# A hybrid encoder block: in its recurrence the low parts of the weights go from GpSimd to VectorE, and three element-wise steps are placed elsewhere

## The chip, the cores and the metric

One core of one Trainium2 chip runs the whole kernel. The metric is the device time of one execution in microseconds (us): the median over runs. The engines are named as in the profile: PE is TensorE, PEld its loading of stationary operands, DVE VectorE, ACT ScalarE, POOL GpSimd, SP SyncE, which here only issues transfers.

## What is computed

The block works on 2048 tokens of width 1024, in float32. After a normalisation one large projection feeds two mixers: latent attention, and a gated linear recurrence (branch B). Their outputs are gated and projected. The change touches branch B alone:

```python
f = lb + (1.0 - lb) * sigmoid(hf)            # lb: one lower bound for each key channel
log_f = log(f);  k_in = 1.0 - f
# for each block of tokens:
cum = cumsum(log_f)
q_dec = q * exp(cum);  k_inv = k_in * exp(-cum);  k_end = k_in * exp(last - cum)
a = where(causal, q_dec @ k_inv.T, 0)
o = a @ v + q_dec @ state                    # state carried from block to block
o = rmsnorm(o, g_hgrn)
```

With s the sigmoid, f is lb + (1 - lb) s, so that 1 - f is (1 - lb)(1 - s). The keys meet only the queries or a state that the queries read later, so a factor 1 - lb for a channel may stand on the queries as well as on the keys.

## The kernel before

Matrix products in float32 are made of three products of a high and a low part of each operand (`three_products`, lines 74 to 76): ACT rounds a tile to its high part, and another engine subtracts that from the tile to get the low part. The program has three stages, one after the other: the input projection, the recurrence with the merge logits (tiles in `bankD`, and names that begin with `d_`), and then latent projections, attention and output.

The recurrence stage is a loop over 16 units. A unit is one pair of heads (128 key channels, one on each partition) by one block of 512 tokens. Beside each unit PE works off 16 groups of three 128x512 products of the merge logits (weights `w_hi`, `w_lo`, whose two buffers are `early_w_*` and `shared_w_*`). These need no result of the recurrence and fill PE; the small products of the unit stand between them at fixed places. `PLACES` says before which group each stands: the turning of the keys (L1692) before group 0, the scores (L1682) and the state updates (L1702) before group 1, the products within a block (L1713) before group 8, those from the states (L1723) before group 9, and the turning of the outputs (L1732) before groups 11 and 12. The first unit has places of its own (`FIRST_PLACES`), later in the unit. In each engine the order is that of the code; semaphores order the engines among themselves.

One unit n on DVE: low part of the turned keys (L1606), masked scores (L1610), the lower bound for unit n + 1 (`lower_bounded`, L1568), state updates and their scan (L1622, L1629), low part of the masked scores (L1633, two instructions, which L1713 on PE waits for), low part of the states (L1635, for L1723), then for unit n + 1 the running sum of log f (`accumulated`, L1575 to L1584), the decayed queries (L1589) and the decayed keys (L1593), then the output scaling of unit n - 1 (`scaled`, L1597 by the inverse norm and L1601 by the gain), and the sums, squares and means of unit n (L1646 to L1651). ACT has the logarithm (L1477), the rounding of the weights (L1506) and of the states (L1533), exponentials (L1481 for the queries, L1490 for the keys, both into the tile `e`), and copies out of PSUM (L1539, L1544). POOL has three low parts and a copy: the weights of unit n + 1 (`split_weights`, L1429), keys and queries (L1443, L1445), values (L1437, L1439). SP loads what is needed two units ahead, once the buffer's last user has signalled, and stores the output.

Of the kernel before, what the change touches and what calls it, by code (L numbers as in the profile page):

```python
# [8 lines left out]
ALU = mybir.AluOpType  # L9
# [97 lines left out]
def input_projection(nc, plain_hi, plain_lo, sums_hi, sums_lo, shared, early, x, g_pre, w_in, b_gate, lb_logits, g_hgrn, ident_d, causal_d,  # L107
# [48 lines left out]
    with ExitStack() as ctx:  # L156
# [238 lines left out]
        with nc.Block() as block:  # L395
# [431 lines left out]
            def _(dve):  # L827
# [179 lines left out]
                dve.wait_ge(next_in, 80)  # L1007
                dve.tensor_scalar(early.f_in[:, 0], early.f_in[:, 0], span[:, 0:1], lb[:, 0:1], ALU.mult, ALU.add).then_inc(lb_step, 1)
                dve.wait_ge(lb_step, 7)

# [240 lines left out]
def merge_logits_and_recurrence(nc, hT_hi, hT_lo, shared, early, own, w_in, projT, hgTok, oB, w_ukv, g_kv):  # L1251
# [13 lines left out]
    with ExitStack() as ctx:  # L1265
# [35 lines left out]
        v_split = sem("v_split")  # L1301
        f_ready = sem("f_ready")
        ln_ready = sem("ln_ready")
# [53 lines left out]
        with nc.Block() as block:  # L1357
# [58 lines left out]
            @block.gpsimd  # L1416
            def _(pool):
                pool.sem_inc(w_split, 1)
                pool.sem_inc(v_split, 1)
                pool.memset(eps[:], EPS).then_inc(const_set, 1)  # L1420
                pool.memset(masked[:], 0.0).then_inc(const_set, 1)
                pool.memset(decay[:], 0.0).then_inc(const_set, 1)
                pool.memset(states[:], 0.0).then_inc(const_set, 1)
                pool.wait_ge(const_set, 4)
                pool.memset(decay[:, :, CPB + 1:], 1.0).then_inc(const_set, 1)

                def split_weights(n, u):
                    pool.wait_ge(w_hi_done, n + 1)
                    pool.tensor_tensor(w_lo[u], w_raw[u], w_hi[u].bitcast(F32), ALU.subtract).then_inc(w_split, 1)  # L1429

                def split_values(n, u, trips):
                    by_head = v_raw[u].rearrange("p t (h n) -> p t h n", n=VD)
                    pool.wait_ge(v_in[u], trips * 16 + 16)
                    if not is_first(n - 1):
                        pool.wait_ge(o_done, n * 2 - 2)
                    pool.sem_inc(waited_pool, 1)
                    pool.tensor_scalar(v[u][:, :, :, 0:VD], by_head, 1.0, None, ALU.mult).then_inc(v_hi, 1)  # L1437
                    pool.wait_ge(v_hi, n)
                    pool.tensor_tensor(v[u][:, :, :, VD:], by_head, v[u][:, :, :, 0:VD].bitcast(F32), ALU.subtract).then_inc(v_split, 1)  # L1439

                def split_unit(n, u):
                    pool.wait_ge(ki_hi, n + 1)
                    pool.tensor_tensor(ki[:, 1], e[:], ki[:, 0].bitcast(F32), ALU.subtract).then_inc(ki_lo, 1)  # L1443
                    pool.wait_ge(qd_hi, n + 1)
                    pool.tensor_tensor(qd[:, 1], q_in2[:, u], qd[:, 0].bitcast(F32), ALU.subtract).then_inc(qd_lo, 1)  # L1445

                split_unit(0, 0)
                split_values(1, 1, 0)
                split_weights(1, 1)
                split_unit(1, 1)  # L1450
                with pool.Fori(0, UNITS // 2 - 1) as i:
                    for u in range(2):
                        split_values(i * 2 + (u + 2), u, i + 1)
                        split_weights(i * 2 + (u + 2), u)
                        split_unit(i * 2 + (u + 2), u)

            @block.scalar
            def _(act):
# [12 lines left out]

                def log_f(n, u):
                    act.wait_ge(f_ready, n + 1)
                    act.wait_ge(ki_lo, n + 1)
                    if not is_first(n):
                        act.wait_ge(ket_turned, n)
                    act.activation(e[:], f_in2[:, u], ACT.Ln).then_inc(ln_ready, 1)  # L1477

# [34 lines left out]

                def unit(n, u, more):
                    act.wait_ge(ket_turned, n + 1)
# [13 lines left out]
                    if more:  # L1529
                        log_f(n + 1, 1 - u)  # L1530
                        round_weights(n + 1, 1 - u)
# [15 lines left out]

                log_f(0, 0)
                exp_up(0)
                act.wait_ge(const_set, 5)  # L1550
                factors(0)
                round_unit(0, 0)
                unit(0, 0, True)
                with act.Fori(0, UNITS // 2 - 1) as i:
                    for u in range(2):
                        unit(i * 2 + (u + 1), 1 - u, True)
                unit(UNITS - 1, 1, False)
                inverse_rms(UNITS - 1)
# [3 lines left out]
            def _(dve):  # L1562

                dve.sem_inc(ki_lo, 1)

                def lower_bounded(pair, u, trips):
                    dve.wait_ge(qf_in[u], trips * 32 + 32)
                    dve.tensor_scalar(f_in2[:, u], f_in2[:, u], span[:, ds(pair, 1)], lb[:, ds(pair, 1)], ALU.mult, ALU.add)\  # L1568
                       .then_inc(f_ready, 1)

# [15 lines left out]

                def decayed_q(n, u):
                    dve.wait_ge(up_ready, n + 1)
                    dve.tensor_tensor(q_in2[:, u], q_in2[:, u], e[:], ALU.mult).then_inc(q_ready, 1)  # L1589

# [3 lines left out]

                def scaled(n):
                    dve.wait_ge(rms_ready, n + 1)
                    dve.tensor_tensor(o_sum[:].rearrange("p h t n -> p (h t) n"), o_sum[:].rearrange("p h t n -> p (h t) n"),  # L1597
                                      rms[:].unsqueeze(2).to_broadcast([P, 2 * TPB, VD]), ALU.mult).then_inc(normed, 1)
                    dve.wait_ge(normed, n + 1)
                    dve.wait_ge(o_stored, n * 16 + 16)  # L1600
                    dve.tensor_tensor(o_out[:].rearrange("p t h n -> p h t n"), o_sum[:],  # L1601
                                      gain[:].unsqueeze(1).unsqueeze(1).to_broadcast([P, 2, TPB, VD]), ALU.mult).then_inc(o_ready, 1)

                def unit(pair, blk, n, more):
                    dve.wait_ge(ket_hi, n + 1)
                    dve.tensor_tensor(ket[:, 1], bank[:, B_TURN[0]], ket[:, 0].bitcast(F32), ALU.subtract).then_inc(ket_lo, 1)  # L1606
                    for hh in range(2):
# [4 lines left out]
                                            bank[:, B_SCORE + hh].rearrange("p (t n) -> p t n", n=P)).then_inc(masked_ready, 1)  # L1612
                    if more:
                        lower_bounded(pair + (blk + 1) // NB, (blk + 1) % 2, pair * (NB // 2) + (blk + 1) // 2)
                    if blk == 0:
# [21 lines left out]
                    if more:  # L1637
                        accumulated(n + 1, (blk + 1) % NB)
                        decayed_q(n + 1, (blk + 1) % 2)
                        decayed_k(n + 1, (blk + 1) % 2)  # L1640
                    if not is_first(n):
                        scaled(n - 1)
                        dve.wait_ge(o_ready, n)
# [9 lines left out]
                dve.sem_inc(w_hi_done, 1)  # L1653
                dve.sem_inc(f_ready, 1)
                dve.memset(inside[:], 1.0).then_inc(inside_set, 1)
# [5 lines left out]
                dve.wait_ge(const_set, 5)  # L1661
                decayed_q(0, 0)
                decayed_k(0, 0)
# [5 lines left out]
                for blk in range(NB):  # L1669
                    unit(PAIRS - 1, blk, (PAIRS - 1) * NB + blk, blk < NB - 1)  # L1670
                scaled(UNITS - 1)

# [1589 lines left out]
```

## Time and profile before

| | |
|---|---|
| median of 3 runs | 2312.72 us (2311.35 to 2313.54) |
| the profiled execution, by the same clock | 2310.02 us |
| its span, first to last instruction | 2308.1 us |
| PE busy | 2150.9 us (93%) |
| DVE, ACT, POOL busy | 1384.1, 1033.5, 462.5 us |
| input projection, until about | 790 us |
| recurrence stage | 790 to 1180 us |
| mean granted clock of PE, whole span | 0.962 |

The profiled execution lasted 1.9 us longer than its span. "Busy" adds up the durations of an engine's instructions; those of PE overlap by modelling, so that a busy PE isn't one at full speed. The granted clock is a share of the full 2.4 GHz: 1.00 is full, 0.50 is 1.2 GHz, and what lies between is a stretch that had both.

### The profile page before, as it was taken

Reading aid. Unit: us, or ns where it says so; the run is one execution under the profiler, and the core shown is the slowest. Engines: PE = TensorE matmul, PEld = TensorE weight load, DVE = VectorE, ACT = ScalarE, POOL = GpSimd, SP = SyncE. Lnnn points to the kernel's source line nnn. Section 1 sums busy time; section 2 is a strip of 40 time slices with the busy share of each in tenths; the row PEclk is TensorE's granted clock in tenths of the full one; section 3 lists DMA queues with packets and bytes.
Section 4 is the critical chain, followed back from the end, with each engine's and each line's share of the span. In section 5 each row is a group of like instructions: output and inputs, shape, how many; then the busy total and the mean of one; then the engine's idle time right before and its main releaser. Section 6 shows DMA issues by size and latency. Waiting matters only on the chain.

```text
span 2308.1 us, 34300 instructions
## 1 busy us (share of the span) xinstructions
PE 2150.9 (93%) x12181; PEld 1820.8 (79%) x12181; DVE 1384.1 (60%) x2192; ACT 1033.5 (45%) x1854; POOL 462.5 (20%) x395
## 2 busy tenths in 40 slices
PE   6999999999999889899978989999999998999998
PEld 5799878878998677777766768778888777778786
DVE  6633445474435466677656657677777767564652
ACT  5322335433224445455443336565666665443441
POOL 3322222442212333333311430000000022000000
PEclk9999999999999979899889999999999999999999
DMA  5432335334324223223166864333212337584651
GB/s 150 120 101 74 105 106 168 101 91 146 101 76 139 74 65 109 73 81 101 55 210 219 274 199 92 71 71 73 53 41 58 74 101 217 160 232 130 201 155 64
DMA packets 264388, 273.14 MB, mean 118 GB/s; under 512 B 38608, under 2 KB 194704, under 8 KB 261776
## 3 DMA queue, kind: packets, MB, share of 16 engines
q1 hardware_dynamic: 253776, 252.36, 38.1%
q0 software_dynamic: 5696, 10.79, 1.8%
q10 hardware_dynamic: 4800, 8.42, 1.0%
q8 instruction: 76, 1.25, 0.2%
q14 instruction: 40, 0.33, 0.0%
HBM read 178.16 MB, written 93.35 MB: 118 GB/s over the span
## 4 chain that ended last, share of the span: by engine, by line
PE 43%; DVE 8%; ACT 5%; DMA 5%; issue 4%; SPq 1%; ACTq 0%; POOL 0%; DVEq 0%; PEldq 0%; POOLq 0%
PE bankE L74 4%; PE bankE L76 3%; PE bankE L75 3%; PE scores L74 3%; PE turn_rest L2650 3%; PE scores L76 2%; PE scores L75 2%; DVE d_a_hl L1633 2%; DMA e_g_in<-gateTok 2%; PE o_acc L2662 2%; PE bankD L74 2%; PE bankD L1723 2%; PE o_acc L2663 2%; PE bankD L76 2%; PE bankD L75 2%
## 5 line engine op out<-in xcount | busy, mean ns | idle before, releaser
L2444 DVE TENSOR_REDUCE small_chunk_min<-scores 128x1 f32<-128x512 f32 (+2 forms) x320 | 181.1, 605 | 34.2 <-PE scores L76 20.0
L865 DVE TENSOR_TENSOR shared_w_lo<-shared_w_raw,shared_w_hi 128x512 fp32r<-128x512 f32 x138 | 109.2, 793 | 139.2 <-ACT shared_w_hi L666 139.0
L2464 ACT ACTIVATE probs<-scores,small_least 128x1024 f32<-128x1024 f32 (+2 forms) x192 | 167.1, 870 | 14.7 <-DVE small_least L2451 13.3
L2598 DVE TENSOR_TENSOR pT<-turn_rest,pT 128x512 fp32r<-128x512 f32 (+2 forms) x208 | 126.2, 625 | 53.0 <-ACT pT L2564 53.0
L666 ACT ACTIVATE shared_w_hi<-shared_w_raw 128x512 fp32r<-128x512 f32 x138 | 84.4, 625 | 152.8 <-POOL shared_w_raw L541 71.9
L74 PE MATMUL scores<-k_sb,q_sb 96*128 96x512 f32 (+2 forms) x320 | 127.2, 397 | 17.3 <-ACT probs L2464 14.5
L2564 ACT ACTIVATE pT<-turn_rest 128x512 fp32r<-128x512 f32 (+2 forms) x208 | 109.5, 548 | 68.9 <-PE turn_rest L2650 49.5
L1084 PE MATMUL bankA<-sums_hi,shared_w_hi 128*128 128x512 f32 x336 | 132.5, 394 | 2.4 <-DVE outs L911 1.7
L1084 PE MATMUL bankA<-sums_hi,shared_w_lo 128*128 128x512 f32 x336 | 131.0, 390 | 0.0
L1084 PE MATMUL bankA<-sums_lo,shared_w_hi 128*128 128x512 f32 x336 | 130.8, 389 | 0.0
L2662 PE MATMUL o_acc<-pT,v_sb 128*128 128x512 f32 (+1 forms) x320 | 125.2, 396 | 4.8 <-DVE pT L2598 3.9
L76 PE MATMUL scores<-k_sb,q_sb 96*128 96x512 f32 (+2 forms) x320 | 119.9, 375 | 0.0
L75 PE MATMUL scores<-k_sb,q_sb 96*128 96x512 f32 (+2 forms) x320 | 119.5, 374 | 0.0
L2663 PE MATMUL o_acc<-pT,v_sb 128*128 128x512 f32 (+1 forms) x320 | 113.3, 366 | 0.0
L74 PE MATMUL bankE<-e_uT,e_wb_hi 128*128 128x512 f32 x256 | 100.9, 394 | 8.7 <-DVE e_wb_lo L3051 6.4
L1084 PE MATMUL bankA<-plain_hi,shared_w_hi 128*128 128x512 f32 x252 | 100.1, 397 | 7.6 <-ACT outs L743 5.1
L2650 PE MATMUL turn_rest<-small_ident,probs 128*128 128x128 f32 x736 | 104.3, 278 | 0.1
L74 PE MATMUL bankE<-e_wo_hi,e_mT 128*128 128x512 f32 x256 | 101.0, 395 | 3.1 <-DVE e_wo_lo L3058 3.1
L76 PE MATMUL bankE<-e_wo_hi,e_mT 128*128 128x512 f32 x256 | 100.2, 391 | 0.0
L2967 POOL TENSOR_TENSOR e_second_branch<-e_second_branch 128x512 f32<-128x512 f32 x4 | 5.1, 1282 | 474.3 <-DMA e_second_branch<-gateTok 474.1
L75 PE MATMUL bankE<-e_wo_lo,e_mT 128*128 128x512 f32 x256 | 100.1, 391 | 0.0
L76 PE MATMUL bankE<-e_uT,e_wb_lo 128*128 128x512 f32 x256 | 99.7, 390 | 0.0
(353 smaller groups left out, 6246.0 us busy)
## 6 DMA issues: line engine op xcount, KB each, us to landing
shared_w_raw<-in_w_in_dram SPq DMA_DIRECT2D x96, 256.0 KB, 3.1
projT<-outs SPq DMA_DIRECT2D x96, 256.0 KB, 2.4
e_l_in<-projT SPq DMA_DIRECT2D x64, 256.0 KB, 4.9
t_raw<-in_w_in_dram SPq DMA_DIRECT2D x24, 512.0 KB, 4.3
x_tile<-in_x_dram SPq DMA_DIRECT2D x16, 512.0 KB, 4.8
projT<-d_stage ACTq DMA_DIRECT2D x32, 256.0 KB, 2.9
knT<-b_out SPq DMA_DIRECT2D x32, 256.0 KB, 3.5
vTok<-b_out SPq DMA_DIRECT2D x32, 256.0 KB, 4.0
```

Source lines behind the costliest of these rows:

```text
L74: pe.matmul(out, a_hi, b_hi, start=first, stop=False)
L75: pe.matmul(out, a_hi, b_lo, start=False, stop=False)
L76: return pe.matmul(out, a_lo, b_hi, start=False, stop=last)
L865: dve.tensor_tensor(slot_lo(u, i), operand(u, i), slot_hi(u, i).bitcast(F32), ALU.subtract).then_inc(w_ready, 1)
L1084: last = pe.matmul(bank[:, b], a[:, k], c[:, k], start=opens and k == 0 and a is wh and c is hh, stop=k == KH - 1 and a is wl, skip_group_ ...
L2444: dve.tensor_reduce(chunk_min[:, i % 2, c:c + 1], scores[:, s_bank(i, c), 0:width(i, c)], AX.X, ALU.min)\
L2464: act.activation(probs[b][:, r, first * BLK:first * BLK + n], src, ACT.Exp, bias=least[:, i % 2:i % 2 + 1], scale=-1.0, accum_out=sums[:, ...
L2564: act.activation(pT[:, at % RING, 0, r0 * P:], turn[TURN_AT[tile] % TURN_RING][:, r0 * P:], ACT.Copy)\
L2598: dve.tensor_tensor(pT[:, at % RING, 1, r0 * P:], turn[TURN_AT[tile] % TURN_RING][:, r0 * P:], pT[:, at % RING, 0, r0 * P:].bitcast(F32), ...
L2650: last = pe.transpose(turn[at % TURN_RING][:, r * P:(r + 1) * P], probs[b][:, r, j * P:(j + 1) * P], ident[:])
L2662: pe.matmul(dst, v_sb[u][:, j], pT[:, at % RING, 0, r0 * P:], start=j == 0, stop=False)
L2663: pe.matmul(dst, v_sb[u][:, j], pT[:, at % RING, 1, r0 * P:], start=False, stop=j == end)\
```

## The change

Four edits, all for the recurrence stage:

1. `split_weights` leaves POOL. DVE does it, as one instruction of 128x1024, right behind the decayed keys.
2. `lower_bounded` is gone, from DVE's unit and once from the end of the input projection. The input tile keeps the sigmoid s. ACT's logarithm gets the lower bound as per-partition scale and bias, and waits for the input itself. The decayed queries are multiplied by `span`, 1 - lb, in the same instruction, which becomes a scalar_tensor_tensor. The decayed keys are computed from s with the instruction as before.
3. `scaled` is cut in two: the scaling by the inverse norm stands ahead of the decayed queries, that by the gain between decayed queries and decayed keys.
4. ACT's loop, which was over two units seven times, is now over the four blocks of a pair of heads, twice, with the first and the last pair written out, since scale and bias need the number of the pair.

```diff
@@ GpSimd
-                def split_weights(n, u):
-                    pool.wait_ge(w_hi_done, n + 1)
-                    pool.tensor_tensor(w_lo[u], w_raw[u], w_hi[u].bitcast(F32), ALU.subtract).then_inc(w_split, 1)
...
                     for u in range(2):
                         split_values(i * 2 + (u + 2), u, i + 1)
-                        split_weights(i * 2 + (u + 2), u)
                         split_unit(i * 2 + (u + 2), u)
@@ ScalarE
-                def log_f(n, u):
-                    act.wait_ge(f_ready, n + 1)
+                def log_f(pair, n, u, trips):
+                    act.wait_ge(qf_in[u], trips * 32 + 32)
                     act.wait_ge(ki_lo, n + 1)
                     if not is_first(n):
                         act.wait_ge(ket_turned, n)
-                    act.activation(e[:], f_in2[:, u], ACT.Ln).then_inc(ln_ready, 1)
+                    act.sem_inc(waited_act, 1)
+                    act.activation(e[:], f_in2[:, u], ACT.Ln, scale=span[:, ds(pair, 1)], bias=lb[:, ds(pair, 1)]).then_inc(ln_ready, 1)
@@ VectorE
-                def lower_bounded(pair, u, trips):
-                    dve.wait_ge(qf_in[u], trips * 32 + 32)
-                    dve.tensor_scalar(f_in2[:, u], f_in2[:, u], span[:, ds(pair, 1)], lb[:, ds(pair, 1)], ALU.mult, ALU.add)\
-                       .then_inc(f_ready, 1)
...
-                    dve.tensor_tensor(q_in2[:, u], q_in2[:, u], e[:], ALU.mult).then_inc(q_ready, 1)
+                    dve.scalar_tensor_tensor(q_in2[:, u], q_in2[:, u], span[:, ds(pair, 1)], e[:], ALU.mult, ALU.mult).then_inc(q_ready, 1)
...
+                def split_weights(n, u):
+                    dve.wait_ge(w_hi_done, n + 1)
+                    dve.tensor_tensor(w_lo[u], w_raw[u], w_hi[u].bitcast(F32), ALU.subtract).then_inc(w_split, 1)
...
-                    if more:
-                        lower_bounded(pair + (blk + 1) // NB, (blk + 1) % 2, pair * (NB // 2) + (blk + 1) // 2)
...
                     if more:
                         accumulated(n + 1, (blk + 1) % NB)
-                        decayed_q(n + 1, (blk + 1) % 2)
+                    if not is_first(n):
+                        scaled_by_rms(n - 1)
+                    if more:
+                        decayed_q(pair + (blk + 1) // NB, n + 1, (blk + 1) % 2)
+                    if not is_first(n):
+                        scaled_by_gain(n - 1)
+                    if more:
                         decayed_k(n + 1, (blk + 1) % 2)
+                        split_weights(n + 1, (blk + 1) % 2)
                     if not is_first(n):
-                        scaled(n - 1)
                         dve.wait_ge(o_ready, n)
```

DVE's queue in the second half of the second unit, before. The names are the tiles written and read: `d_cum` the running sum, `early_q_in` the queries, `d_e` the keys, `d_o_sum` and `d_o_out` the output.

```order
L1635 TENSOR_TENSOR d_s_hl<-d_states,d_s_hl 128x8x64
L1575 SCALAR_TENSOR_TENSOR d_cum<-d_inside,d_carry,d_e 128x512
L1580 COPY d_gsum<-d_cum 128x8
L1581 COPY d_carry<-d_cum 128x1
L1584 TENSOR_TENSOR d_cum<-d_cum,d_gsum 128x8x32
L1589 TENSOR_TENSOR early_q_in<-early_q_in,d_e 128x512
L1593 SCALAR_TENSOR_TENSOR d_e<-early_f_in,d_e 128x512
L1597 TENSOR_TENSOR d_o_sum<-d_o_sum,d_rms 128x512
L1601 TENSOR_TENSOR d_o_out<-d_o_sum,shared_gain 128x2x4x64
L1646 TENSOR_TENSOR d_o_sum<-bankD,d_o_lo 128x256 x2
L1649 TENSOR_TENSOR d_o_lo<-d_o_sum 128x512
```

The same place of the changed kernel, whose line numbers differ:

```order
L1628 TENSOR_TENSOR d_s_hl<-d_states,d_s_hl 128x8x64
L1564 SCALAR_TENSOR_TENSOR d_cum<-d_inside,d_carry,d_e 128x512
L1569 COPY d_gsum<-d_cum 128x8
L1570 COPY d_carry<-d_cum 128x1
L1573 TENSOR_TENSOR d_cum<-d_cum,d_gsum 128x8x32
L1590 TENSOR_TENSOR d_o_sum<-d_o_sum,d_rms 128x512
L1578 SCALAR_TENSOR_TENSOR early_q_in<-early_q_in,shared_small,d_e 128x512
L1596 TENSOR_TENSOR d_o_out<-d_o_sum,shared_gain 128x2x4x64
L1582 SCALAR_TENSOR_TENSOR d_e<-early_f_in,d_e 128x512
L1586 TENSOR_TENSOR early_w_lo<-early_w_raw,early_w_hi 128x1024
L1645 TENSOR_TENSOR d_o_sum<-bankD,d_o_lo 128x256 x2
L1648 TENSOR_TENSOR d_o_lo<-d_o_sum 128x512
```

The two scalings have moved up, one on either side of the decayed queries, and the weights' low part stands where they stood.

POOL's loop body for one unit, before: values, weights, keys, queries.

```order
L1437 TENSOR_SCALAR early_v<-early_v_raw 128x8x64
L1439 TENSOR_TENSOR early_v<-early_v_raw,early_v 128x8x64
L1428 REGISTER_ALU
L1429 TENSOR_TENSOR early_w_lo<-early_w_raw,early_w_hi 128x1024
L1443 TENSOR_TENSOR d_ki<-d_e,d_ki 128x512
L1445 TENSOR_TENSOR d_qd<-early_q_in,d_qd 128x512
```

And in the changed kernel:

```order
L1429 TENSOR_SCALAR early_v<-early_v_raw 128x8x64
L1431 TENSOR_TENSOR early_v<-early_v_raw,early_v 128x8x64
L1434 REGISTER_ALU
L1435 TENSOR_TENSOR d_ki<-d_e,d_ki 128x512
L1437 TENSOR_TENSOR d_qd<-early_q_in,d_qd 128x512
```

The instruction of 128x1024 between values and keys is gone from POOL, and nothing takes its place.

## Rows read from the trace of the kernel before

**Rows 1.** The page: span and number of instructions.

```profile
span 2308.1 us, 34300 instructions
```

**Rows 2.** Stretches of the recurrence: length, PE busy, granted clock, DMA share, GB/s.

```profile
822.68:1159.58 336.90, 309.15 (x2184) 0.88 0.30 86
990.37:1016.54 26.17, 24.18 (x157) 0.80 0.41 122
1016.54:1038.00 21.46, 19.49 (x157) 1.00 0.17 47
1159.58:1178.67 19.09, 19.09 (x156) 1.00 0.12 40
```

**Rows 3.** Waits from 822.68 us on: us in total, times, longest.

```profile
PE bankD L1713 <- DVE d_a_hl L1633: 27.8, 14, 2.0
```

**Rows 4.** PE's timeline, unit from 1016.54: start, us, instruction, idle before.

```profile
1017.77 1.56 PE L1682 MATMUL bankD<-d_qd,d_ki 64*128 64x128 f32 x24
...
1025.28 0.39 PE L76 MATMUL bankD<-plain_hi,shared_w_lo 128*128 128x512 f32 x1
1027.63 2.00 PE L1713 MATMUL bankD<-d_a_hl,d_v 128*128 128x128 f32 x16 [1.97 <-DVE d_a_hl L1633]
...
1030.31 1.97 PE L1723 MATMUL bankD<-d_qd,d_s_hl 64*128 64x64 f32 x32
...
1033.70 0.60 PE L1732 MATMUL bankD<-shared_ident,d_o_fm 128*128 128x128 f32 x4
```

**Rows 5.** DVE's timeline in the same unit.

```profile
1019.49 1.35 DVE L1610 COPY_PREDICATED d_masked<-shared_causal,bankD 128x512 f32<-128x512 int32 x2 [0.99 <-PE bankD L1682]
1020.73 0.53 DVE L1568 TENSOR_SCALAR early_f_in<-early_f_in,shared_small 128x512 f32<-128x512 f32 x1
...
1022.73 1.49 DVE L1629 TENSOR_TENSOR_SCAN d_states<-d_states,d_decay 128x640 f32<-128x640 f32 x1 [0.20 <-ACT d_states L1526]
1024.14 3.44 DVE L1633 TENSOR_TENSOR d_a_hl<-d_masked,d_a_hl 128x512 fp32r<-128x512 f32 x2
...
1031.14 0.69 DVE L1589 TENSOR_TENSOR early_q_in<-early_q_in,d_e 128x512 f32<-128x512 f32 x1 [0.70 <-ACT d_e L1481]
1032.53 0.69 DVE L1593 SCALAR_TENSOR_TENSOR d_e<-early_f_in,d_e 128x512 f32<-128x512 f32 x1 [0.70 <-ACT d_e L1490]
...
1035.88 0.43 DVE L1646 TENSOR_TENSOR d_o_sum<-bankD,d_o_lo 128x256 f32<-128x256 f32 x1 [0.43 <-ACT d_o_lo L1544]
```

**Rows 6.** POOL's timeline in the same unit.

```profile
1024.33 2.70 POOL L1429 TENSOR_TENSOR early_w_lo<-early_w_raw,early_w_hi 128x1024 fp32r<-128x1024 f32 x1 [8.77 <-ACT early_w_hi L1506]
1034.20 1.59 POOL L1443 TENSOR_TENSOR d_ki<-d_e,d_ki 128x512 fp32r<-128x512 f32 x1 [7.18 <-ACT d_ki L1496]
```

**Rows 7.** DVE and PE in the last unit, timeline from 1159 us.

```profile
1162.50 1.36 DVE L1610 COPY_PREDICATED d_masked<-shared_causal,bankD 128x512 f32<-128x512 int32 x2 [0.96 <-PE bankD L1682]
...
1165.76 1.49 DVE L1629 TENSOR_TENSOR_SCAN d_states<-d_states,d_decay 128x640 f32<-128x640 f32 x1 [0.65 <-ACT d_states L1526]
1167.17 1.27 DVE L1633 TENSOR_TENSOR d_a_hl<-d_masked,d_a_hl 128x512 fp32r<-128x512 f32 x2
...
1168.30 0.39 PE L76 MATMUL bankD<-plain_hi,shared_w_lo 128*128 128x512 f32 x1
1168.53 1.97 PE L1713 MATMUL bankD<-d_a_hl,d_v 128*128 128x128 f32 x16
```

**Rows 8.** ACT's timeline in the unit from 1016.54.

```profile
1024.25 1.20 ACT L1533 ACTIVATE d_s_hl<-d_states 128x512 fp32r<-128x512 f32 x1
...
1032.53 1.09 ACT L1539 ACTIVATE d_o_fm<-bankD 128x512 f32<-128x512 f32 x2
```

**Rows 9.** Durations in ns, min/median/max, by tile and by line, 785 to 1200 us.

```profile
L1584 DVE TENSOR_TENSOR d_cum<-d_cum,d_gsum x16: 424/426/427, 792.4 to 1146.8; 128x256 f32<-128x256 f32 x16
...
L1464 ACT ACTIVATE d_stage<-bankD,shared_small x32: 681/686/690, 822.1 to 1179.2; 128x512 f32<-128x512 f32 x32
```

**Rows 10.** PE in the first unit, timeline.

```profile
809.85 3.67 PE L1713 MATMUL bankD<-d_a_hl,early_v 128*128 128x128 f32 x16 [4.65 <-DVE d_a_hl L1633]
```

More of the change, by code:

```diff
@@ L1007, in _ @@
                 dve.wait_ge(next_in, 80)
-                dve.tensor_scalar(early.f_in[:, 0], early.f_in[:, 0], span[:, 0:1], lb[:, 0:1], ALU.mult, ALU.add).then_inc(lb_step, 1)
-                dve.wait_ge(lb_step, 7)
             @block.tensor
@@ L1301, in merge_logits_and_recurrence @@
         v_split = sem("v_split")
-        f_ready = sem("f_ready")
         ln_ready = sem("ln_ready")
@@ L1417, in _ @@
             def _(pool):
-                pool.sem_inc(w_split, 1)
                 pool.sem_inc(v_split, 1)
@@ L1448, in _ @@
                 split_values(1, 1, 0)
-                split_weights(1, 1)
                 split_unit(1, 1)
@@ L1512, in inverse_rms, with unit @@
                     act.activation(rms[:], logm[:], ACT.Exp, scale=-0.5).then_inc(rms_ready, 1)
-                def unit(n, u, more):
+                def unit(pair, blk, n, more):
+                    u = blk % 2
                     act.wait_ge(ket_turned, n + 1)
@@ L1529, in unit @@
                     if more:
-                        log_f(n + 1, 1 - u)
+                        log_f(pair + (blk + 1) // NB, n + 1, 1 - u, pair * (NB // 2) + (blk + 1) // 2)
                         round_weights(n + 1, 1 - u)
@@ L1546, in unit @@
                     logits(n, 0)
-                log_f(0, 0)
+                log_f(0, 0, 0, 0)
                 exp_up(0)
@@ L1552, in _ @@
                 round_unit(0, 0)
[L1553 to L1557, printed above, removed]
+                for blk in range(NB):
+                    unit(0, blk, blk, True)
+                with act.Fori(1, PAIRS - 1) as pair:
+                    for blk in range(NB):
+                        unit(pair, blk, pair * NB + blk, True)
+                for blk in range(NB):
+                    unit(PAIRS - 1, blk, (PAIRS - 1) * NB + blk, blk < NB - 1)
                 inverse_rms(UNITS - 1)
@@ L1585, in accumulated, with decayed_q @@
                        .then_inc(mid_ready, 1)
-                def decayed_q(n, u):
+                def decayed_q(pair, n, u):
                     dve.wait_ge(up_ready, n + 1)
-                    dve.tensor_tensor(q_in2[:, u], q_in2[:, u], e[:], ALU.mult).then_inc(q_ready, 1)
+                    dve.scalar_tensor_tensor(q_in2[:, u], q_in2[:, u], span[:, ds(pair, 1)], e[:], ALU.mult, ALU.mult).then_inc(q_ready, 1)
                 def decayed_k(n, u):
@@ L1593, in decayed_k, with scaled_by_rms @@
                     dve.scalar_tensor_tensor(e[:], f_in2[:, u], 1.0, e[:], ALU.subtract, ALU.mult).then_inc(kd_ready, 1)
-                def scaled(n):
+                def split_weights(n, u):
+                    dve.wait_ge(w_hi_done, n + 1)
+                    dve.tensor_tensor(w_lo[u], w_raw[u], w_hi[u].bitcast(F32), ALU.subtract).then_inc(w_split, 1)
+                def scaled_by_rms(n):
                     dve.wait_ge(rms_ready, n + 1)
@@ L1598, in scaled, with scaled_by_gain @@
                                       rms[:].unsqueeze(2).to_broadcast([P, 2 * TPB, VD]), ALU.mult).then_inc(normed, 1)
+                def scaled_by_gain(n):
                     dve.wait_ge(normed, n + 1)
@@ L1653, in _ @@
                 dve.sem_inc(w_hi_done, 1)
-                dve.sem_inc(f_ready, 1)
+                dve.sem_inc(w_split, 1)
                 dve.memset(inside[:], 1.0).then_inc(inside_set, 1)
@@ L1661, in _ @@
                 dve.wait_ge(const_set, 5)
-                decayed_q(0, 0)
+                decayed_q(0, 0, 0)
                 decayed_k(0, 0)
@@ L1670, in _ @@
                     unit(PAIRS - 1, blk, (PAIRS - 1) * NB + blk, blk < NB - 1)
-                scaled(UNITS - 1)
+                scaled_by_rms(UNITS - 1)
+                scaled_by_gain(UNITS - 1)
             @block.tensor
```

## The prediction

> **What bounds the kernel now.** I began with the page, whose span is 2308.1 us [rows 1], and cut it into stages, since every edit stands in the recurrence, 790 to 1180 us. There I asked which wait ends last on PE, the engine with the most work. The table of waits gives one of weight: from 822.68 us on PE waits 14 times for the low part of the masked scores (DVE, L1633), 27.8 us in all [rows 3]. The 15th unit after the first has no such wait.
>
> Then I cut the stage at the turning of the keys, the start of a unit on PE. From 822.68 to 1159.58 us there are 14 units in 336.90 us, 24.06 each, at a mean granted clock of 0.88 [rows 2]. They are of two kinds. Six last 21.5 us at clock 1.00, like the one from 1016.54; the other eight last (336.90 - 6 x 21.46) / 8 = 26.0 us on average, like the one from 990.37 with 26.17 at 0.80 [rows 2]. The clock goes to 1.2 GHz only right behind the wait for L1633, in those eight. So a unit loses twice: the wait itself, and in eight of 14 units a stretch at half clock.
>
> Next the wait's cause, in the unit from 1016.54. PE's last large product ahead of L1713 starts at 1025.28; they follow each other every 0.23 us, so PE is free at 1025.51, and L1713 starts at 1027.63 [rows 4]: 2.12 us lost. DVE's two subtractions start at 1024.14 and end at 1027.58, 3.44 us for two [rows 5]. At 1024.33 POOL begins the weights' low part and runs 2.70 us, to 1027.03 [rows 6]. In the last unit no weights are left to split and there is no lower bound to apply: the same two subtractions take 1.27 us, and L1713 starts at 1168.53, 0.23 us behind the product before it, with no wait [rows 7]. This is the changed unit nearly as it will be, already in the trace. Its L1713 comes at the clock 1.00, and the clock stays there to the end of the unit [rows 2].
>
> **The change part by part.** *Weights' low part off POOL.* With L1633 at 1.27 instead of 3.44, the scores' low part ends 2.17 us earlier. From the start of L1610 to the end of L1633 the fast unit takes 1027.58 - 1019.49 = 8.09 us, the last unit 1168.44 - 1162.50 = 5.94 [rows 5, 7]. So in the unit from 1016.54 it would end at 1025.43, and PE is free at 1025.51. The 2.12 us go, and what is left of slack is 0.08 us: it just fits.
>
> *Lower bound gone.* Its 0.53 us [rows 5] are worth nothing on this path: the scan behind it waits for ACT's state updates, 0.20 us with it and 0.65 us in the last unit without it [rows 5, 7]. At the end of the input projection the one instruction lies beside ACT's last work; nothing. On ACT the logarithm gets two per-partition operands. The trace has none such; The nearest rows are an activation of the same shape without operands (half of 1.09 us for two, in rows that overlap, so at least 0.55 [rows 8]) and one with a per-partition bias, 0.69 [rows 9]. The bounds are 0.55 and 0.8, and I take 0.69; the old logarithm takes about 0.6. Behind it in ACT's queue is the rounding of the states, which ends at 1025.45 [rows 8]; the states' low part takes 1.0 us from there, and PE wants it 2.68 us behind the start of L1713 [rows 4], at 1028.2. That is 1.7 us of slack, and 0.1 is hidden in it. The wait for the input in place of DVE's signal costs nothing: the loads are issued two units ahead.
>
> *Output scaling.* Two instructions of about 0.69 us stand in the two gaps of 0.70 us in which DVE waits for ACT's exponentials [rows 5]. They fill them exactly; between 0 and 0.1 us of delay each. Behind stand the decayed keys, on whose heels ACT's copy of the outputs follows. In the fast unit that copy starts at 1032.53 and its first half is ready at about 1033.1, while the turning of the outputs starts at 1033.70 [rows 4, 8]: 0.6 us of slack, and both sides move up by the same 2.1 us. Hidden.
>
> *Weights' low part on DVE.* A subtraction of 256 elements takes 0.43 us [rows 9], one of 512 takes 0.69 [rows 5], so 1024 take 0.69 + 2 x 0.26 = 1.2; bounds are 1.2 and POOL's 2.70 [rows 6]. I take 1.2. It starts at 1033.2 - 2.1 = 1031.1 and ends at 1032.3. Queued behind it is the second sum of the outputs, which started at 1035.88 [rows 5], now 1033.8 (the first 0.9 us earlier): hidden, even at 1.7 us. If it took 2.7 us, the first sum would be late by 0.9 and the second not; PE wants them at the next unit's start, 1035.9, when they have been done for 1.7 us. PE needs the weights then too: 3.6 us of slack. SP loads into the raw buffer once the split has signalled; that load stood behind the store of the output, which itself waited for the scaling by the gain, and both can now go out earlier.
>
> *POOL.* Its keys' low part starts at 1034.20 and takes 1.59 us [rows 6]; one for the queries follows, up to 1.6 more: done by 1037.4, now by 1035.3. The scores of the next unit want it at 1036.0 + 1.23 = 1037.2 [rows 4]: 1.9 us of slack. Can the new subtraction on DVE hold these up? The row says that a DVE subtraction and POOL's can't run beside each other: L1633 took 3.44 us where 1.27 is its own time, and ended 0.55 us behind POOL's end [rows 5, 6]. Moved up with the rest, POOL starts at 1032.1 and DVE ends at 1032.3: POOL loses 0.2 of its 1.9 us. The Trainium skill (SBUF — State Buffer, "Who interferes with whom") has this as a rule: a DVE instruction with two SBUF inputs and a GpSimd instruction that reads SBUF share a port, and whichever starts first holds it for the whole instruction. It speaks against the edit, since the weights' subtraction still has two SBUF inputs, and by it the loss is moved rather than removed; by the rule the sum is less only if POOL's slack is used up, which the rows deny.
>
> *Sum.* 14 units of 2.12 us are 29.7 us. Half clock: 336.90 - 14 x 21.46 = 36.5 us; if no wait is left ahead of L1713, all of it goes. Together 66.1 us: 14 units of 24.06 become 19.34, and the last unit's 19.09 plus 0.23 is 19.32 [rows 2]. The first unit: PE waited 4.65 us [rows 10]; DVE's pair was just as slow there, so 2.15 us go, but 2.5 remain, and I leave the half clock behind it (3.67 us for L1713). Total 68.3 us. Profiled execution: 2310.0 - 68.3 = 2241.7. Its time stands 2.7 us under the median of the runs, 2312.7, so by the median 2244.4; I say 2244.
>
> **The rivals.** *Half clock stays in some units.* For: behind L1713 and L1723 PE has 48 small products in 4.6 us that stream little, and nothing shows that the wait alone turned the clock down; six of 14 units with the same wait kept it. Against: the last unit, and 48 small products of the scores and updates at each unit's start, behind which the clock never fell. Each such unit costs 36.5 / 8 = 4.6 us; five give 2267, all eight 2281. Chance 0.14.
>
> *The wait goes elsewhere.* Either ACT or DVE is late by more than its slack (0.08 us at L1713, 0.6 at L1732), by the filled gaps or added register work. A wait of 1 us in each unit, with no clock loss, costs 14: 2258; one as long as that removed leaves it at 2313. Chance 0.1, of which 0.02 for no change.
>
> *It doesn't do what it says:* L1633 was slow for another reason than POOL. The last unit also lacks the lower bound and the next unit's work. Against: the end of L1633 follows POOL's end by 0.55 us, and POOL has nothing else there. It would give 2313. Chance 0.02.
>
> *Slower.* ACT's logarithm with two per-partition operands is far dearer than its rows. It stands in front of the states' rounding; its delay reaches PE at L1723 beyond 1.7 us, and is as bad as the old loss (66.1 / 14 = 4.7 us a unit) from 6.4 us on; at 7.5 us it gives 2313 + 14 x 1.1 = 2328. The rows say 0.55 to 0.8. Chance 0.02, with anything else that ends above.
>
> **How the numbers follow.** The likeliest case, 0.72, is 2244, its own range 2239 (the first unit keeps its clock too) to 2250 (0.4 us of small delays a unit). For 8 in 10 I reach to five units with half clock: 2238 to 2267. 0.2% is 4.6 us, about what a measurement of this kernel can tell from no change. Faster is the likeliest, the clock rival and most of the moved wait, 0.95; same 0.03; slower 0.02.
>
> **What would show it.** Right: L1633's successor at 0.68 us for each of its two, PE without a wait ahead of the products within a block, units of 19.3 to 19.5 us, a granted clock of 1.00 from the second unit on, the weights' subtraction on DVE at 1.2 us, POOL's keys at 1.3 to 1.6. Wrong: units of two kinds at clock 0.8 and 1.0 (first rival), a wait of PE for the copied or summed outputs or the states (second), or a logarithm over 0.8 us (last).

## The result and the profile after

| | before | changed |
|---|---|---|
| median | 2312.03 us (2307.65 to 2313.54, 4 runs) | 2241.47 us (2236.52 to 2249.32, 4 runs) |
| ratio, 95% interval | | 0.9701 (0.9667 to 0.9735) |
| span of the profiled execution | 2308.1 us | 2247.5 us |
| its own time | 2310.02 us | 2249.32 us |

The kernel is 70.6 us faster by the medians, and 60.7 us by the profiled executions; that of the changed kernel is the slowest of its four. The page of the changed kernel, its head and section 1 (busy us, share, instructions):

```profile
span 2247.5 us, 34185 instructions
PE 2119.2 (94%) x12181; PEld 1797.7 (80%) x12181; DVE 1364.3 (61%) x2191; ACT 1033.7 (46%) x1854; POOL 425.1 (19%) x380
```

PE has the same 12181 instructions. Its busy time fell by 32 us only, since what left is partly idle time. The stretches of its recurrence, each cut at the turning of the keys as in [rows 2] (length, PE busy, granted clock, DMA share, GB/s):

```profile
818.91:843.72 24.81, 24.81 (x157) 0.76 0.35 93
843.72:1094.98 251.26, 251.26 (x2030) 1.00 0.35 102
1017.65:1037.01 19.36, 19.36 (x157) 1.00 0.38 109
```

From 843.72 to 1094.98 us stand 13 units of 19.33 us at a granted clock of 1.00, with PE busy from end to end. In [rows 2] a unit had 24.06 us on average. One unit, the second, is still long. In the timelines of PE, DVE, ACT and POOL for the unit from 1017.65, the answers to [rows 4 to 6] and [rows 8] are:

```profile
1026.38 0.39 PE L76 MATMUL bankD<-plain_hi,shared_w_lo 128*128 128x512 f32 x1
1026.61 1.99 PE L1713 MATMUL bankD<-d_a_hl,d_v 128*128 128x128 f32 x16
...
1023.86 1.49 DVE L1622 TENSOR_TENSOR_SCAN d_states<-d_states,d_decay 128x640 f32<-128x640 f32 x1 [0.65 <-ACT d_states L1518]
1025.27 1.27 DVE L1626 TENSOR_TENSOR d_a_hl<-d_masked,d_a_hl 128x512 fp32r<-128x512 f32 x2
1026.69 1.11 DVE L1628 TENSOR_TENSOR d_s_hl<-d_states,d_s_hl 128x512 fp32r<-128x512 f32 x1 [0.16 <-ACT d_s_hl L1525]
...
1030.41 0.75 DVE L1578 SCALAR_TENSOR_TENSOR early_q_in<-early_q_in,shared_small,d_e 128x512 f32<-128x512 f32 x1 [0.21 <-ACT d_e L1472]
1031.87 0.69 DVE L1582 SCALAR_TENSOR_TENSOR d_e<-early_f_in,d_e 128x512 f32<-128x512 f32 x1
1032.48 1.22 DVE L1586 TENSOR_TENSOR early_w_lo<-early_w_raw,early_w_hi 128x1024 fp32r<-128x1024 f32 x1
1035.32 1.32 DVE L1648 TENSOR_TENSOR d_o_lo<-d_o_sum 128x512 f32<-128x512 f32 x1
...
1023.80 0.82 ACT L1468 ACTIVATE d_e<-early_f_in,shared_small 128x512 f32<-128x512 f32 x1
...
1033.54 1.30 POOL L1435 TENSOR_TENSOR d_ki<-d_e,d_ki 128x512 fp32r<-128x512 f32 x1 [13.63 <-ACT d_ki L1487]
1034.80 1.29 POOL L1437 TENSOR_TENSOR d_qd<-early_q_in,d_qd 128x512 fp32r<-128x512 f32 x1
```

The two subtractions for the scores (now L1626) take 1.27 us and end at 1026.54. L1713 starts 0.23 us behind the product ahead of it, without a wait, and 0.07 us behind their end. The scan of the states waits 0.65 us for ACT, as in the last unit of before [rows 7]: what the lower bound had taken became waiting. The weights' subtraction takes 1.22 us on DVE, and POOL's keys start 0.16 us before its end by this profile. The logarithm on ACT takes 0.82 us, more than I had allowed; it pushes the states' low part back by 0.16 us, which is hidden. POOL idles 13.63 us ahead of the keys.

The contention isn't gone from the unit. The square of the outputs (L1648) has two inputs in SBUF too. Here it takes 1.32 us where 0.69 is its own time (in the run with the first edit alone, below), and ends 0.55 us behind the end of POOL's queries (1036.64 against 1036.09). PE doesn't wait for it.

### The profile page after: what moved, and what is told of

Read it like the earlier page. It is cut to its first block, busy times and chain, and to the rows that moved or that the text cites. A ratio compares the mean times of both kernels' runs of the same rounds, so it can differ in the third digit from the quotient of the medians.

```text
span 2247.5 us, 34185 instructions
## 1 busy us (share of the span) xinstructions
PE 2119.2 (94%) x12181; PEld 1797.7 (80%) x12181; DVE 1364.3 (61%) x2191; ACT 1033.7 (46%) x1854; POOL 425.1 (19%) x380
## 4 chain that ended last, share of the span: by engine, by line
PE 46%; DMA 5%; DVE 4%; ACT 4%; issue 3%; SPq 1%; POOL 1%; ACTq 0%; DVEq 0%; POOLq 0%
PE bankE L74 4%; PE bankE L76 4%; PE bankE L75 4%; PE scores L74 3%; PE bankD L74 3%; PE turn_rest L2650 3%; PE scores L75 3%; PE scores L76 3%; PE bankD L76 3%; PE bankD L75 3%; PE o_acc L2662 2%; PE o_acc L2663 2%; DMA e_g_in<-gateTok 2%; PE turn_first L2650 2%; ACT probs L2464 1%
## 5 line engine op out<-in xcount | busy, mean ns | idle before, releaser
L74 PE MATMUL scores<-k_sb,q_sb 96*128 96x512 f32 (+2 forms) x320 | 129.3, 404 | 20.2 <-ACT probs L2464 15.0
L76 PE MATMUL scores<-k_sb,q_sb 96*128 96x512 f32 (+2 forms) x320 | 121.6, 380 | 0.0
L75 PE MATMUL scores<-k_sb,q_sb 96*128 96x512 f32 (+2 forms) x320 | 121.6, 380 | 0.0
L74 PEld LDWEIGHTS scores<-k_sb,q_sb 96*128 96x128 f32 x320 | 63.5, 198 | 45.8 <-ACT probs L2464 29.3
```

The lines of the kernel that those rows point to most:

```text
L74: pe.matmul(out, a_hi, b_hi, start=first, stop=False)
L75: pe.matmul(out, a_hi, b_lo, start=False, stop=False)
L76: return pe.matmul(out, a_lo, b_hi, start=False, stop=last)
```

## The experiments

The runs fall into three groups, each on a chip of its own, with runs of the kernel before on that chip. The changed kernel ran in each of them again, with ratios of 0.9694 (0.9652 to 0.9737), 0.9685 (0.9658 to 0.9712) and 0.9703 (0.9676 to 0.9731). I give unit lengths on PE from the profiled execution beside each time, since single executions of one kernel differ by up to 22 us (before: 2305.41 to 2327.84 us on one chip), while the changed kernel's units, from the third on, repeat within 0.1 us.

**The first edit alone.** The subtraction of the weights moves to DVE behind the decayed keys of the kernel before; all else stays.

```diff
...
                         decayed_k(n + 1, (blk + 1) % 2)
+                        split_weights(n + 1, (blk + 1) % 2)
                     if not is_first(n):
                         scaled(n - 1)
```

> The kernel before with the first edit alone: the low part of the weights on VectorE behind the decayed keys; lower bound, logarithm and output scaling as before. My theory: the whole gain is the wait for the scores' low part and the half clock behind it, so this run is as fast as the changed kernel (ratio to before 0.97, some 2242 us), units of 19.3 to 19.4 us with granted clock 1.00, no wait of PE ahead of the products within a block. It shows two subtractions at 1.27 us although the lower bound still stands ahead of them. Rival, the other edits matter: the output scaling now stands behind the weights' subtraction and makes the sums of the outputs late by 0.5 to 0.9 us; PE waits for them at the start of a unit, units of 20 us or more, 2250 to 2260 us.

Measured: 2253.82 us (2250.99 to 2255.87), ratio 0.9735 (0.9694 to 0.9776), beside 2244.57 us for the changed kernel on that chip. The rival was right in the time, the unit and the wait. Of my theory two parts held: the clock is at full from the second unit on, and the wait for the scores is gone. But a unit lasts 281.10 / 14 = 20.08 us and not 19.33, and PE has a new wait. One stretch, the wait in it, and two lines of the tile `d_o_sum` (ns min/median/max) of this kernel:

```profile
821.12:1102.22 281.10, 273.21 (x2184) 1.00 0.32 97
...
PE bankD L1691 <- DVE d_o_sum L1644: 8.2, 14, 0.9
...
L1594 DVE TENSOR_TENSOR d_o_sum<-d_o_sum,d_rms x16: 684/1776/1785, 836.9 to 1121.9; 128x512 f32<-128x512 f32 x16
L1598 DVE TENSOR_TENSOR d_o_out<-d_o_sum,shared_gain x16: 693/1562/1670, 838.7 to 1122.6; 128x512 f32<-128x512 f32 x16
```

Here L1594 and L1598 are the two scalings. They take 1.78 and 1.56 us where 0.68 and 0.69 are their own times. The timelines of DVE and POOL in one unit show why (L1647 is the square of the outputs, here at its own time):

```profile
1036.43 1.22 DVE L1590 TENSOR_TENSOR early_w_lo<-early_w_raw,early_w_hi 128x1024 fp32r<-128x1024 f32 x1
1037.57 1.77 DVE L1594 TENSOR_TENSOR d_o_sum<-d_o_sum,d_rms 128x512 f32<-128x512 f32 x1
1039.48 1.56 DVE L1598 TENSOR_TENSOR d_o_out<-d_o_sum,shared_gain 128x512 f32<-128x512 f32 x1
1041.87 0.69 DVE L1647 TENSOR_TENSOR d_o_lo<-d_o_sum 128x512 f32<-128x512 f32 x1
...
1037.50 1.29 POOL L1438 TENSOR_TENSOR d_ki<-d_e,d_ki 128x512 fp32r<-128x512 f32 x1 [13.75 <-ACT d_ki L1489]
1038.76 1.74 POOL L1440 TENSOR_TENSOR d_qd<-early_q_in,d_qd 128x512 fp32r<-128x512 f32 x1
1040.46 1.93 POOL L1432 TENSOR_SCALAR d_v<-d_v_raw 128x512 fp32r<-128x512 f32 x1
```

Pushed back by 1.2 us, the first scaling starts 0.07 us behind POOL's keys, and ends 0.55 us behind their end (1038.79). That is the same distance as in [rows 5, 6]. The second falls beside POOL's queries and ends 0.54 us behind their end (1041.04 against 1040.50). The sums of the outputs come late, and PE waits for them. So the contention that the first edit removes at one place comes back at another.

**All but the first edit.** The changed kernel with the weights' subtraction on POOL, in its old place.

```diff
...
                         split_values(i * 2 + (u + 2), u, i + 1)
+                        split_weights(i * 2 + (u + 2), u)
                         split_unit(i * 2 + (u + 2), u)
```

> The changed kernel with the first edit undone: the low part of the weights back on GpSimd; lower bound folded, output scaling in two places, VectorE's queue shorter than before. My theory: no gain, ratio 0.99 to 1.00 (2295 to 2313 us); the two subtractions take 3.4 us again, PE waits 2.1 us a unit and half the units have a stretch at half clock. Rival, the pair was slow or late for the work that the lower bound put ahead of it: then a good part of the 70 us appears here.

Measured: 2310.1 us (2306.43 to 2315.15), ratio 0.9988 (0.9967 to 1.0008). The rival falls. Two neighbouring units of this kernel, and the subtractions for the scores:

```profile
919.80:946.02 26.22, 24.25 (x158) 0.80 0.33 94
946.02:967.48 21.46, 19.47 (x158) 1.00 0.27 82
...
L1629 DVE TENSOR_TENSOR d_a_hl<-d_masked,d_a_hl x32: 664/676/2859, 808.1 to 1166.4; 128x512 fp32r<-128x512 f32 x32
```

These are the two kinds of unit of before, to a few hundredths [rows 2], and the longest subtraction again has 2.86 us. So neither the lower bound nor the place of the scalings had made it slow.

**POOL writes at that place but doesn't read.** In the kernel before, POOL's subtraction is replaced by a memset of the same tile (the weights' low part is then zero; PE's products are the same in number and place, but the result lacks its share).

```diff
                     pool.wait_ge(w_hi_done, n + 1)
-                    pool.tensor_tensor(w_lo[u], w_raw[u], w_hi[u].bitcast(F32), ALU.subtract).then_inc(w_split, 1)
+                    pool.sem_inc(waited_pool, 1)
+                    pool.memset(w_lo[u].bitcast(F32), 0.0).then_inc(w_split, 1)
```

> The kernel before, but GpSimd's subtraction for the weights' low part is replaced by a memset of the same tile of 128x1024 (the low part of the weights is left out of the products, being zero), in the same place of its queue. If VectorE's subtraction is held by GpSimd reading SBUF, the pair takes 1.27 us and the time is about 2242 us. If any work of GpSimd at that place holds it, the pair ends 0.6 to 0.7 us behind the memset's end, some 1.8 us for the two, PE waits about 0.5 us a unit, and the time is 2250 us or more, depending on the clock.

Measured: 2244.71 us, one run. The timelines of DVE and POOL:

```profile
1021.24 1.27 DVE L1634 TENSOR_TENSOR d_a_hl<-d_masked,d_a_hl 128x512 fp32r<-128x512 f32 x2
...
1021.50 0.96 POOL L1430 MEMSET early_w_lo<- 128x1024 f32 x1 [5.43 <-ACT early_w_hi L1507]
```

A unit of this kernel:

```profile
858.93:878.28 19.35, 19.35 (x157) 1.00 0.35 107
```

The memset lies inside the pair (1021.50 to 1022.46, against 1021.24 to 1022.51), and the pair takes 1.27 us. So it is the reading of SBUF by POOL that holds DVE. That is the rule of the Trainium skill (SBUF — State Buffer, "Who interferes with whom"), by which a GpSimd instruction that only writes doesn't contend with a DVE instruction of two SBUF inputs; here the trace agrees. All four edits together gain what this one replacement gains, as far as one run can tell: its units last 19.35 us, and its time is that of the changed kernel on this chip (2244.57 us).

**The wait alone, without contention.** In the changed kernel the products within a block are placed one, two or three groups earlier on PE, so that PE waits for subtractions which are as fast as ever (at most 689 ns each in the three runs).

```diff
-    PLACES = 0, 1, 1, 8, 9, (11, 12)
+    PLACES = 0, 1, 1, 5, 9, (11, 12)
```

Three groups early:

> The changed kernel with the products within a block placed before group 5 instead of 8, nothing else. They come three groups (2.05 us) earlier on PE while VectorE's subtractions stay as fast as they are, so PE waits 2.0 to 2.1 us a unit, with no contention anywhere. If the wait alone sets off the half clock: about half of the units at granted clock 0.80 and the whole gain gone, 2300 to 2313 us. If the half clock came from something else, the wait costs only its own length: 14 x 2.05 = 29 us, 2271 us.

One group early (7 in the place of 8):

> The changed kernel with the products within a block before group 7: one group (0.68 us) earlier, so PE waits 0.6 to 0.7 us a unit. If a short wait leaves the clock alone: 15 x 0.6 = 9 us, 2251 us, all units at clock 1.00. If any wait there sets off the half clock in some units: 4.6 us more for each such unit, 2265 us or more.

Two groups early (6), one run:

> The changed kernel with the products within a block before group 6, two groups early, so that PE waits 1.2 us a unit; the runs with one and with three groups early had 0.5 us with the clock at full in every unit from the second on, and 1.84 us with every second unit in part at half clock. If the wait alone counts and half clock comes in part of the units: units of two kinds, 20.7 and some 22 us, 2265 to 2275 us. If it stays away: 20.7 us each, 2242 + 14 x 1.3 = 2260 us.

| groups early | wait a unit | a unit at clock 1.00 | units at clock under 1.00 | time |
|---|---|---|---|---|
| 0 (changed kernel) | none | 19.33 us | 1 of 14 (the second) | 2239.08 us (2233.55 to 2248.05), ratio 0.9685 (0.9658 to 0.9712) |
| 1 | 0.5 us | 20.03 us | 0 of 14 | 2256.93 us (2245.22 to 2263.39), ratio 0.9749 (0.9712 to 0.9786) |
| 2 | 1.2 us | 20.71 us | 1 of 14 | 2263.62 us (another chip) |
| 3 | 1.85 us | 21.39 us | 7 of 14 | 2284.05 us (2282.67 to 2286.9), ratio 0.9887 (0.9856 to 0.9918) |

The wait is PE's idle time by the profile; a unit at full clock grew by 0.7 us for each group, somewhat more than that. The second unit is in these counts: it was at 0.86 with three groups early and at 1.00 with one and two. Two neighbours of the run with three groups early, and one long unit of the run with two:

```profile
864.06:887.06 23.00, 21.16 (x157) 0.93 0.35 93
887.06:908.48 21.42, 19.57 (x158) 1.00 0.34 95
...
943.18:965.42 22.24, 21.08 (x157) 0.92 0.32 95
```

So a wait of PE sets off the half clock also where nothing holds the subtractions, and in half the units when it is 1.85 us. Why it is every second unit, no run shows. With one group early the clock did as expected, but the time came out 6 us over the 2251 us; its four executions spread over 18 us. The recurrence doesn't account for it; in the profiled execution the stage behind took 1158.0 us, the longest of all profiles. My expectation for three groups failed in size. It had the whole gain gone, and 45 us of the 73 on that chip went. A long unit costs 23.00 - 21.42 = 1.6 us there and 26.17 - 21.46 = 4.7 us before [rows 2]. The stretches at the two edges of half clock, with three groups early and then in the kernel before (the unit from 990.37), show how long it lasted:

```profile
874.00:875.00 1.00, 1.00 (x10) 0.94 0.00 0
878.00:879.00 1.00, 1.00 (x5) 0.85 0.06 18
...
1003.00:1004.00 1.00, 1.00 (x7) 0.60 0.00 0
1013.00:1014.00 1.00, 1.00 (x7) 0.78 0.52 155
```

Between them the clock is at 0.50 throughout. That makes 3.4 us of half clock in one and 10.2 us in the other, and half of each, 1.7 and 5.1 us, is about what the unit lost. What differs besides is what follows the wait: four groups of 128x512 products stand between L1713 and the 32 products of 64 columns (L1723) in this run, and one group in the kernel before. I take this for the reason that the clock came back sooner, but no run changes it alone.

**Other places in the first unit.**

```diff
-    FIRST_PLACES = 8, 11, 11, 14, 15, (16, 16)
+    FIRST_PLACES = 8, 10, 10, 15, 16, (16, 16)
```

> The changed kernel with other places in the first unit: scores and updates before group 10 instead of 11, products within a block before group 15 instead of 14, those from the states before group 16 instead of 15. PE's wait there is 2.5 us now, behind which the clock is at half from the first unit's products to the second unit's updates (24.8 us for the second unit where 19.3 is usual). Scores one group earlier bring the subtractions 0.7 us forward, and one group more stands ahead of the wait: 1.1 us is left of it. If the clock then holds: 1.4 us of wait, 3 to 4 us of the first unit and 5.5 us of the second, some 9 us faster than the changed kernel, ratio 0.966. Rival: with two groups less cover behind, PE waits for the states' low part and the outputs' copies at the end of the first unit, the clock falls anyway, and it is no faster, or 1 to 2 us slower.

Measured: 2243.64 us (2237.48 to 2250.43), ratio 0.9713 (0.9686 to 0.9740), beside 2239.08 us and 0.9685 (0.9658 to 0.9712) for the changed kernel: no faster, as the rival had it (the two intervals overlap). PE's waits in its first unit, 18.86 us long:

```profile
PE bankD L1713 <- DVE d_a_hl L1626: 1.2, 1, 1.2
PE bankD L1732 <- ACT d_o_fm L1531: 1.1, 1, 1.1
PE bankD L1682 <- POOL d_qd L1437: 0.8, 1, 0.8
```

The one wait of 2.5 us became three, and a fourth of 1.0 us ends the unit. The first unit is 3.6 to 4.3 us shorter than in the changed kernel's profiles (22.41 to 23.14 us), but the clock falls at its end, and the second lasts 24.66 us.

**The third edit undone, and the second.** First the changed kernel with both scalings behind the weights' subtraction:

```diff
...
                         decayed_k(n + 1, (blk + 1) % 2)
                         split_weights(n + 1, (blk + 1) % 2)
                     if not is_first(n):
+                        scaled_by_rms(n - 1)
+                        scaled_by_gain(n - 1)
```

> The changed kernel with the third edit undone: both scalings of the output stand behind the weights' subtraction again. In the run with the first edit alone, the scalings took 1.77 and 1.56 us there instead of 0.69, beside GpSimd's low parts of the keys and queries, and PE waited 0.6 us a unit for the sums of the outputs. If the place of the scalings is what that cost: the same here, units of 20.0 to 20.1 us, some 10 us slower than the changed kernel. If it was the lower bound's instruction on VectorE: units of 19.33 us, the changed kernel's time.

Then the first and the third edit without the second:

```diff
-                    act.activation(e[:], f_in2[:, u], ACT.Ln, scale=span[:, ds(pair, 1)], bias=lb[:, ds(pair, 1)]).then_inc(ln_ready, 1)
+                    act.activation(e[:], f_in2[:, u], ACT.Ln).then_inc(ln_ready, 1)
...
+                    if more:
+                        lower_bounded(pair + (blk + 1) // NB, (blk + 1) % 2, pair * (NB // 2) + (blk + 1) // 2)
```

> The first and the third edit without the second: lower bound by an instruction of its own on VectorE, plain logarithm, plain decayed queries. If the place of the scalings is all that was missing in the run with the first edit alone: units of 19.33 us and the time of the changed kernel, within 2 us. If the lower bound's 0.53 us on VectorE matter: units longer by up to 0.5 us, up to 8 us slower.

Measured: 2263.47 us (2260.15 to 2266.3), ratio 0.9799 (0.9780 to 0.9818), and 2239.72 us (2239.68 to 2247.11), ratio 0.9703 (0.9679 to 0.9727), beside 2243.77 us and 0.9703 for the changed kernel. With the scalings behind, 13 units last 20.25 us each and PE waits for the sums again:

```profile
848.51:1111.77 263.26, 253.69 (x2029) 1.00 0.32 96
...
PE bankD L1688 <- DVE d_o_sum L1641: 8.8, 12, 0.8
```

Without the second edit the units are 19.33 us and PE waits for nothing in them. So the third edit is worth 0.75 us a unit once the first is made (from the run with the first edit alone), and 0.92 us with the second made too. The second is worth nothing in the changed kernel. Where the scalings stand behind, it even costs: units of 20.25 us with it and 20.08 without, and ratios of 0.9799 and 0.9735 whose intervals don't meet (the fourth edit goes with the second in these runs; which instruction costs the 0.17 us was not tried).

I had expected units of 20.0 to 20.1 us and some 10 us for the scalings behind. The time is 20 us over the changed kernel's. The 13 units explain 12. In the two profiled executions the whole distance was 13.8 us: 12.1 in the recurrence, 3.0 ahead of it and 1.3 less behind it. The other 6 us between the medians no profile shows.

## Why the prediction was right

**The wait and its cause.** Right. Behind the first unit, 14 waits and 27.8 us [rows 3] became none. The cause was POOL's reading beside DVE's two inputs; the run with all but the first edit and the one with the memset show it from both sides.

**The last unit as the model.** Right to a few hundredths. 19.32 us were worked out from it, and 13 units of 19.33 came. The slack of 0.08 us at L1713 was measured as 0.07.

**Half clock.** Right from the third unit on: 36.5 us were to go, and no such unit is left. Wrong for the second unit. I had ended the half clock behind the first unit's wait with that unit; in the profiled execution it runs into the second, 24.81 us at 0.76. Here the first rival came in for one unit. In the changed kernel's four profiled executions the second unit had 24.81, 19.38, 24.75 and 24.37 us, so that this term is 5 us or nothing, by the execution; I had expected the repeats to agree within 1 us from that unit on. The last three:

```profile
818.71:838.09 19.38, 19.38 (x157) 1.00 0.44 113
821.59:846.34 24.75, 24.75 (x156) 0.76 0.37 94
821.07:845.44 24.37, 24.37 (x156) 0.78 0.36 95
```

**The sum.** In the profiled executions PE's last unit began 64.6 us sooner (1094.98 against 1159.58), 1.2 us of which it had before its first turning of keys. The remaining 63.4 us stand against 68.3 forecast: 60.8 against 66.1 for the 14 units, all of the gap being the second one, and 2.5 against 2.15 for the first. What follows took 1152.5 us where it had been 1148.5, so the span fell by 60.6. Of the profiled execution I had said 2241.7 us, and it took 2249.32. By the medians the time fell by 70.6 us, and 2241.47 stands beside the 2244 forecast. That closeness is partly luck: the profiled execution of before was 2.0 us under its median, that of the changed kernel 7.9 us over its own, and what the second unit lost isn't in the forecast at all. Part of such distances comes from the stage behind the recurrence, whose code is the same in every run. In four profiled executions of the changed kernel it took 1148.0 to 1154.3 us, and 1141.8 to 1158.0 us over all profiles. No profile shows the executions that make up the medians.

**The weights' subtraction.** Right: 1.2 us forecast, 1.22 measured. "Hidden" was right in this kernel, but it needs the third edit. I had priced the scalings as filling two gaps of 0.70 us, at no gain or loss. What they do there is stay clear of POOL's keys and queries. Behind the subtraction they would take 3.3 us instead of 1.4, which the run with the first edit alone shows; that was not in my working. I had asked whether the weights' subtraction would hold up POOL, and not whether POOL would hold up the instructions pushed back behind it.

**ACT and DVE forms.** The logarithm with two per-partition operands takes 0.817 us, above my bound of 0.8 and well above the 0.69 taken. I had named a logarithm over 0.8 us as a sign of being wrong, so that sign appeared, without its consequence. The decayed queries take 0.752 us for 0.69. Both were hidden, the first by 1.7 us of slack.

**The rivals.** The wait that goes elsewhere didn't come, but would have without the third edit, at 0.92 us a unit (0.75 us with the first edit alone). The slower case stayed far off.

## What to carry to other kernels

When an instruction of VectorE with two SBUF inputs lasts several times as long as its siblings, look at what GpSimd runs in that time, and count what the moved work will meet at its new place too: here the first edit alone lost 0.75 us a unit to the same contention elsewhere. A short wait of TensorE can cost more than its length, by the clock behind it, so price it with the long units and not with the wait alone. Where the last turn of a loop lacks the work that an edit removes, the trace of before already holds the changed turn, though not what the moved work meets at its new place: the last unit had no work of POOL, and so showed nothing of what the scalings ran into.

## What was unexpected of the hardware

- A wait of 0.5 us in each unit left the clock at full in all of 14, one of 1.2 us in all but one, one of 1.85 us in half; the cost of a long unit was 1.6 us (3.4 us at half clock) with four groups of large products behind L1713 and 4.7 us (10.2 us at half clock) with one.
- With the wait in place, long and short units took turns (26.2, 21.5, 26.2, 21.5 us) through nearly the whole loop, in the kernel before and in that with all but the first edit.
- A logarithm of 128x512 takes 0.63 us without and 0.82 us with per-partition scale and bias.
- Executions of the changed kernel on one chip spread over 14.5 us (2233.55 to 2248.05), though its units from the third on repeat within 0.1 us.
- A DVE instruction held by POOL shows as a long one, not as idle time, and ended 0.54 to 0.55 us behind the end of POOL's instruction in the four cases shown: the scores' low part before (1027.58 against 1027.03), both scalings with the first edit alone, and the square of the outputs in the changed kernel.
